# Two arriving and three split weight buffers in place of four and two

## The reference

```python
h = rmsnorm(x, g_norm[0])
(fq, fk, fv, ff, cq, ckv, kpe, hq, hf, hi, hg, ga, gb, gc) = split(h @ w_in)
# three branches: forgetting attention, latent attention, gated recurrence (HGRN)
merged = (sigmoid(ga) * (o_fox @ w_branch[0]) + sigmoid(gb) * (o_mla @ w_branch[1])
          + sigmoid(gc) * (o_hg @ w_branch[2]))
x = x + rmsnorm(merged @ w_out, g_norm[1])
mk, mv = mem_prompt @ w_mem_k, mem_prompt @ w_mem_v          # 256 memory tokens
x = x + rmsnorm(attend(rmsnorm(x) @ w_xq, mk, mv) @ w_xo, g_norm[3])
u = square(relu(rmsnorm(x) @ w_up)) @ w_down                 # hidden 4096
x = x + rmsnorm(u, g_norm[5])
```

## Time and profile before

| | |
|---|---|
| runs of the kernel before | 2767.38, 2757.2, 2757.35 us; median 2757.35 |
| profiled execution | 2763.47 us, its span 2761.4 us |
| mean granted TensorE clock | 0.962 of full speed |
| TensorE busy | 2558.0 us, 93% of the span |
| GpSimd busy | 1211.4 us, 44% |
| VectorE, ScalarE busy | 1043.5 us, 38%; 708.0 us, 26% |
| HBM traffic | 77 GB/s over the span |

### The profile page before, as it was taken

How to read it: one execution, slowest core, us unless ns; L and a number is a source line. 1 busy time by engine, 2 the same in 40 slices (tenths; PEclk the granted TensorE clock), 3 DMA queues, 4 the chain that set the end, 5 groups by cost and what they waited for, 6 DMA issues and landing times.

```text
span 2761.4 us, 43281 instructions
## 1 busy us (share of the span) xinstructions
PE 2558.0 (93%) x18670; PEld 2395.3 (87%) x18670; DVE 1043.5 (38%) x1596; ACT 708.0 (26%) x1571; POOL 1211.4 (44%) x700
## 2 busy tenths in 40 slices
PE   8899999998888899999898999999998887999997
PEld 7878977997788789999897799689887887999997
DVE  5441222477523341221363311324775244311223
ACT  2053133135412430011121522322253134210111
POOL 4312510664364245656543034126643742555563
PEclk9999999999999999999999999999999998999999
DMA  5313410330232123233234123113302421232321
GB/s 177 100 48 97 112 41 16 85 89 24 77 124 85 39 62 92 85 92 86 77 102 122 41 79 92 41 29 87 81 16 85 133 83 32 70 91 85 92 85 56
DMA packets 354533, 214.59 MB, mean 78 GB/s; under 512 B 22316, under 2 KB 347240, under 8 KB 353704
## 3 DMA queue, kind: packets, MB, share of 16 engines
q1 hardware_dynamic: 320632, 179.86, 22.8%
q10 hardware_dynamic: 33712, 31.97, 3.7%
HBM read 196.09 MB, written 15.71 MB: 77 GB/s over the span
## 4 chain that ended last, share of the span: by engine, by line
PE 83%; DVE 8%; ACT 3%; issue 3%; POOL 2%; DMA 0%; SPq 0%; DVEq 0%; ACTq 0%; POOLq 0%
PE psum L720 20%; PE psum L718 20%; PE psum L719 20%; PE psum L789 2%; PE psum L828 2%; PE psum L730 2%; POOL w_lo L652 2%; PE psum L1114 1%; PE psum L1002 1%; PE psum L925 1%; PE psum L748 1%; PE psum L749 1%; PE psum L750 1%; PE psum L763 1%; DVE square_sum_and_rs L2023 1%
## 5 line engine op out<-in xcount | busy, mean ns | idle before, releaser
L650 POOL CAST w_hi<-w_raw 128x1024 fp32r<-128x1024 f32 x318 | 338.5, 1064 | 1406.7 <-PE psum L720 1229.3
L652 POOL TENSOR_TENSOR w_lo<-w_raw,w_hi 128x1024 fp32r<-128x1024 f32 x318 | 811.2, 2551 | 25.5
L718 PE MATMUL psum<-h_hi,w_hi 128*128 128x272 f32 x2720 | 793.4, 292 | 16.3 <-POOL w_lo L652 12.5
L720 PE MATMUL psum<-h_hi,w_lo 128*128 128x272 f32 x2720 | 790.7, 291 | 0.0
L719 PE MATMUL psum<-h_lo,w_hi 128*128 128x272 f32 x2720 | 786.0, 289 | 0.0
L718 PEld LDWEIGHTS psum<-h_hi,w_hi 128*128 128x128 f32 x2720 | 516.4, 190 | 21.1 <-issue 18.0
L719 PEld LDWEIGHTS psum<-h_lo,w_hi 128*128 128x128 f32 x2720 | 516.7, 190 | 0.7 <-issue 0.5
L720 PEld LDWEIGHTS psum<-h_hi,w_lo 128*128 128x128 f32 x2720 | 515.2, 189 | 0.0
L718 PE MATMUL psum<-r_hi,w_hi 128*128 128x272 f32 x1696 | 494.8, 292 | 17.0 <-DVE r_lo L2125 11.6
L720 PE MATMUL psum<-r_hi,w_lo 128*128 128x272 f32 x1696 | 496.6, 293 | 0.0
L719 PE MATMUL psum<-r_lo,w_hi 128*128 128x272 f32 x1696 | 492.5, 290 | 0.0
(11 more groups left out here) (380 smaller groups left out, 3591.7 us busy)
## 6 DMA issues: line engine op xcount, KB each, us to landing
w_raw<-in_w_in SPq DMA_DIRECT2D x116, 512.0 KB, 3.8
w_raw<-in_w_up SPq DMA_DIRECT2D x64, 512.0 KB, 4.0
w_raw<-in_w_down SPq DMA_DIRECT2D x64, 512.0 KB, 4.0
w_raw<-in_w_branch SPq DMA_DIRECT2D x24, 512.0 KB, 3.4
w_raw<-in_w_out SPq DMA_DIRECT2D x16, 512.0 KB, 4.1
x_kept<-x SPq DMA_DIRECT2D x2, 2176.0 KB, 8.9
x<-x_kept SPq DMA_DIRECT2D x2, 2176.0 KB, 10.5
fKc<-in_cache_fox_k ACTq DMA_DIRECT2D x4, 1024.0 KB, 8.2
```

The source lines that it names most:

```text
L650: nc.gpsimd.tensor_copy(w_hi[:, at % SPLIT, :], raw[:, at % RAW, :]).then_inc(high_split, 1)
L652: nc.gpsimd.tensor_tensor(w_lo[:, at % SPLIT, :], raw[:, at % RAW, :], w_hi[:, at % SPLIT, :].bitcast(F32), ALU.subtract).then_inc(weights ...
L718: pe.matmul(dst, whi[:, k, :], hi[:, k, c0:c1], start=k == 0, stop=False)
L720: last = pe.matmul(dst, wlo[:, k, :], hi[:, k, c0:c1], start=False, stop=k == kt - 1)
```

## The change

The number of arriving buffers goes from four to two and that of split buffers from two to three. One arriving buffer is 4 KB in each partition, one split buffer twice that (a high and a low part), so the sum is 16 + 16 KB before and 8 + 24 KB after. The two first loads are still issued ahead of the loop, and a literal 2 stands there now, since that number was SPLIT's before.

```diff
-RAW, SPLIT = 4, 2
+RAW, SPLIT = 2, 3
...
         def sp_layer(sp, l):
-            for s in range(0 if l else SPLIT, N_SLOTS):
+            for s in range(0 if l else 2, N_SLOTS):
                 load_slot(sp, l, s)
```

## The result

| | before | after |
|---|---|---|
| median, 12 runs each, same chip | 2766.55 us (2757.2 to 2776.59) | 2752.32 us (2749.93 to 2761.96) |
| ratio, 95% interval | | 0.9949 [0.9933, 0.9965] |
| span of the profiled execution | 2761.4 us | 2747.9 us |
| mean granted clock | 0.962 | 0.961 |

The kernel gains 14.2 us where the sum said 23.3. 2752.32 lies 1.3 us above the upper end of the wide range (2751), 9.3 above that of the forecast's own (2743), and 18 above the forecast. Half of the 18 is the base: two of the three runs behind 2757.35 were low ones among the kernel's executions, and 2766.55 - 23.3 would have been 2743.3. The other 9.1 us are a term of the sum that was wrong, and the traces show where.

A forecast was written before the change was run, and what follows sets the result against it. TensorE, busy 93% of the span, was taken to set the end. Projections 20.6 plus recurrence's start 2.7 gave 23.3 us, so 2757.35 - 23.3 = 2734 us; own range 2730 to 2743, wide range 2728 to 2751.

The forecast's parts named there:

- Projections, 20.6 us: Output and memory projections: third split buffer removes TensorE's stalls for low parts, 10.3 us a layer, 20.6 in all.
- Two arriving buffers, 0: Weight loads, issued two splits back instead of four: still land early enough, cost 0; other end 3 us a layer.
- Rival (a): Memory stretch: the two arriving buffers pace it, loads landing in 5.8 us give 2742 us, in 6.7 2755; chance 0.13.
- (d): MLP: landing time of loads paces it, at 9.4 us a load 72 us lost, 2806 us in total; chance 0.05.
- The recurrence's start, 2.7 us: Start of each recurrence: an earlier split lets GpSimd's clearings end before VectorE needs them, 1.35 us a layer, 2.7 in all.
- The recurrence's end, 0: End of each recurrence: the moved split's subtraction starts after VectorE's product and costs 0; other end 4.4 us.
- Rival (b): End of each recurrence: the moved split holds VectorE's product, 2.2 us a layer, gain 18.9, 2738 us; chance 0.15.
- Rival (c): Behind the projections: residual's return or norm sets the pace, only the recurrence's gain is left, about 2755 us; chance 0.07.

The follow-up runs named there:

- experiment 2: Changed kernel with split buffers back from three to two, so only the two arriving buffers differ from the kernel before: 2767.3 us, ratio to before 1.0002.
- experiment 4: Changed kernel, but in the output and memory projections a split waits for the slot two back; third split buffer used everywhere else: 2775.43 us, ratio to before 1.0031.

## Why the prediction was right in three terms and wrong in the fourth

- **Projections, 20.6 us: right.** Six pairs take 53.12 and 53.11 us where 53.2 was worked out, and the twelve waits are gone. The stall per pair, taken from the windows and not from the bare waits, was the right measure: the waits alone (17.8) would have been 3 us short.
- **Two arriving buffers, 0: right**, by experiment 2. The late load was there as foreseen, behind the residual's return; GpSimd waited 3.11 and 4.03 us for it, more than the 2 that were named, and TensorE not at all. Rival (a) falls with it, and (d): nothing in the MLP got slower.
- **The recurrence's start, 2.7 us: right in sum (2.8), partly by luck.** TensorE's gap there went from 2.97 to 1.53 us in both layers, as foreseen (1.4 for 1.35), but a later wait grew by 1.0 and 0.9 us, and the clock behind both decided what was left: 0.8 in one layer, 2.0 in the other.
- **The recurrence's end, 0: wrong, and it is the whole miss of the sum.** The step that failed is "VectorE still finishes the held product until 706.75, which holds the cast, so I take the later one, 0". The mechanism was seen and the window named (the subtraction to start between 707.5 and 708.0, the product at 707.73); the choice between its ends was a toss, and it was treated as settled. The product's turn came 3.61 us after the one before it (707.73 - 704.12), which from 705.92 is 709.53; the subtraction began at 709.52. Rival (b) is what happened, in both layers, with a chance of 0.15 where the window gave each side about half.
- **And (b) itself was priced at half.** 2.2 us a layer was the product's delay; TensorE stood 2.3 longer. What it left out is what TensorE does after standing 2.4 us: 5.80 us for work of 4.35, and in layer 1 a whole 6.47 us at the lower level. 4.4 us became 8.9. The kernel before had such stops: 2.97 us at 623.97, with a granted clock of 0.68 in the 16 us from 624, in which there were more stops. So a row to price it by was there and wasn't looked for.

```profile
624.00:640.00 16.00, 13.88 (x81) 12.68 (x81) 10.44 (x22) 9.87 (x24) 7.70 (x7) 0.68 0.02 6
```

- **Rival (c), the won time is waited for elsewhere: no.** Nothing behind the projections gave it back: the difference of -4.42 us at the end of layer 0's pairs is still -4.14 at layer 1's recurrence.
- **The base.** A median of three runs was taken as the kernel's time; twelve runs put it 9 us higher. The span and its 2763.47 us were nearer.

What stays open: why the clock fell for the whole stretch in layer 1 and for part of it in layer 0 after stops of the same 2.38 us (in experiment 4 it fell for a part of it in both layers), and the drops at 229 us, which took a different time in each of the three traces shown.

## What to carry to other kernels

A deeper buffer moves work earlier, and what was the wait of an idle engine becomes that engine running beside another: list where the freed instructions land, and for each the operations of the neighbours that read the same memory. When such a landing is a race of a few tenths of a microsecond, give both sides their half, and price the loser with the stop *and* with what the clock does behind the stop. Where one buffer helps in one stretch and harms in another, its use can be chosen slot by slot: a hold on one split and a reordered one took the gain from 0.5% to 1.1%.

## What the hardware showed that was not expected

- In these rows the instruction that started first, be it by hundredths of a microsecond, wasn't held and the other one was: subtractions that start 0.14 us (709.52 against 709.66) or 0.23 us (705.69 against 705.92) ahead of the product hold it until 0.3 us past their own end (2.58 and 2.63 us in place of 0.42); one that starts 0.02 us behind VectorE's (738.72 against 738.70) leaves it its 0.72 us and takes 2.91 itself. GpSimd's clearings beside the product cost nothing (0.42).
- The cast, with one input, is slowed and slows only a little: 1.25 to 1.50 us beside VectorE in place of 1.04, and VectorE's product at 709.18 took 0.56 us in place of 0.42.
- A stop of 2.4 us of TensorE cost up to 2.9 us more behind it, by the lower clock, more than the stop itself.
